# Making the rated feed-forward input in the first turn of the loop instead of the first two

## What is computed

```python
def conv_ffn(h, w_up, conv_w, conv_b, w_down):
    u = h @ w_up
    u = conv_b + sum(conv_w[j] * causal_shift(u, CONV_WIDTH - 1 - j) for j in range(CONV_WIDTH))
    gate, val = jnp.split(u, 2, axis=-1)
    return (jax.nn.silu(gate) * val) @ w_down
...
        x = x + conv_ffn(rms_norm(x, norm_ffn_g[l]), ffn_w_up[l], ffn_conv_w[l],
                         ffn_conv_b[l], ffn_w_down[l])
```

## Time and profile before

| what | us |
|---|---|
| median of 3 runs | 1028.18 (1027.68 to 1029.34) |
| the profiled execution | 1028.37 |
| its span, first to last instruction | 1026.6 |
| TensorE busy | 1008.1 (98%) |
| VectorE busy | 816.6 (80%) |
| ScalarE busy | 616.9 (60%) |

### The profile page before, as it was taken

One profiled execution on the slowest core, in us unless ns is written; L12 is line 12 of the kernel. 1 busy time (PEld: TensorE's weight loads), 2 busy tenths in 40 slices (PEclk: granted clock), 3 DMA queues, 4 the chain that ended last, 5 costly groups with the idle time before them and its releaser, 6 DMA issues.

```text
span 1026.6 us, 22212 instructions
## 1 busy us (share of the span) xinstructions
PE 1008.1 (98%) x8278; PEld 932.0 (91%) x8278; DVE 816.6 (80%) x1365; ACT 616.9 (60%) x967; POOL 11.9 (1%) x30
## 2 busy tenths in 40 slices
PE   8999999999999999999999999999999999999997
PEld 7998988899999999999999989789999999998886
DVE  6799763897797898878778996649977878888785
ACT  7964333656556665666689533246656565667665
POOL 0000000100000000000000000010000000000000
PEclk9999999999999999999999999999999999999999
DMA  8452342335545565555544534224445545565554
GB/s 301 148 182 103 104 146 81 114 111 178 162 154 179 180 209 183 189 185 184 191 142 145 185 99 144 88 74 142 139 153 167 182 164 185 172 219 185 192 192 152
DMA packets 46392, 164.42 MB, mean 160 GB/s; under 512 B 5888, under 2 KB 6064, under 8 KB 46304
## 3 DMA queue, kind: packets, MB, share of 16 engines
q1 hardware_dynamic: 44640, 160.19, 46.8%
q0 software_dynamic: 800, 1.33, 0.6%
q10 hardware_dynamic: 864, 1.63, 0.5%
HBM read 161.56 MB, written 1.05 MB: 158 GB/s over the span
## 4 chain that ended last, share of the span: by engine, by line
PE 86%; DVE 9%; ACT 2%; issue 2%; DMA 1%; SPq 0%; DVEq 0%; ACTq 0%
PE psum L471 85%; DVE sb_lo L1317 2%; ACT sb_rw L927 1%; DVE sb_inv L1566 1%; DVE sb_inv L1525 1%; DMA sb_x<-x_t 1%; DVE sb_inv L1528 1%; PE psum L789 1%; ACT sb_hh L927 0%; DVE sb_rw L1609 0%; DVE sb_yf L1590 0%; DVE sb_qb L1375 0%; ACT sb_hi L927 0%; DVE sb_rw L1496 0%; DVE sb_inv L1502 0%
## 5 line engine op out<-in xcount | busy, mean ns | idle before, releaser
L927 ACT ACTIVATE sb_hi<-sb_raw 128x1024 fp32r<-128x1024 f32 (+1 forms) x298 | 310.4, 1052 | 170.7 <-PE psum L471 161.2
L1317 DVE TENSOR_TENSOR sb_lo<-sb_raw,sb_hi 128x1024 fp32r<-128x1024 f32 x296 | 358.0, 1219 | 53.2 <-ACT sb_hi L927 52.9
L471 PE MATMUL psum<-sb_hh,sb_hi 128*128 128x256 f32 x1184 | 344.2, 291 | 3.2 <-DVE sb_hl L1324 2.1
L471 PE MATMUL psum<-sb_hl,sb_hi 128*128 128x256 f32 x1184 | 335.3, 283 | 0.0
L471 PE MATMUL psum<-sb_hh,sb_lo 128*128 128x256 f32 x1184 | 335.1, 283 | 0.0
L471 PE MATMUL psum<-sb_o,sb_hi 128*128 128x256 f32 (+1 forms) x1376 | 276.0, 314 | 1.3 <-DVE sb_o L1338 1.3
L471 PEld LDWEIGHTS psum<-sb_hh,sb_hi 128*128 128x128 f32 x1184 | 227.0, 192 | 17.9 <-issue 10.9
L471 PEld LDWEIGHTS psum<-sb_o,sb_hi 128*128 128x128 f32 x1376 | 224.1, 191 | 14.6 <-DVE sb_o L1338 1.7
L471 PEld LDWEIGHTS psum<-sb_hl,sb_hi 128*128 128x128 f32 x1184 | 227.3, 192 | 0.8 <-issue 0.5
L471 PEld LDWEIGHTS psum<-sb_hh,sb_lo 128*128 128x128 f32 x1184 | 227.2, 192 | 0.0
L471 PE MATMUL psum<-sb_o,sb_lo 128*128 128x256 f32 x880 | 193.9, 283 | 0.0
(11 more groups left out here) (187 smaller groups left out, 1027.7 us busy)
## 6 DMA issues: line engine op xcount, KB each, us to landing
sb_raw<-w_stream SPq DMA_DIRECT2D x299, 512.0 KB, 3.3
sb_pm<-mix_par ACTq DMA_DIRECT2D x2, 512.5 KB, 3.4
y_t<-sb_rw SPq DMA_DIRECT2D x4, 256.0 KB, 2.1
sb_cf<-const_f SPq DMA_DIRECT2D x1, 550.0 KB, 9.3
sb_pm<-mix_par SPq DMA_DIRECT2D x1, 512.5 KB, 10.9
sb_raw<-w_stream SPq DMA_DIRECT2D x2, 256.0 KB, 4.4
sb_x<-x_t ACTq DMA_DIRECT2D x2, 256.0 KB, 4.4
sb_x<-x_t SPq DMA_DIRECT2D x1, 512.0 KB, 6.7
```

Of the source, the lines that this page charges most:

```text
L471: return pe.matmul(out, lhsT, rhs, start=start, stop=stop, skip_group_check=True)
L927: return act.activation(out, in_, func, scale=scale, bias=bias, **kw)
L1317: tt(lo[:, s, :], raw[:, s, :], hi[:, s, :].bitcast(F32), ALU.subtract).then_inc(lo_done, 1)
```

## The change

`PLAIN_TURNS` goes from 2 to 1, so `RATED_FROM` goes from 10 to 6, and the loop of the program begins with the second turn. The rated input has to be ready four tiles earlier, and its steps move:

- `rate` 0 and 1 stand ahead of the first turn, 2 and 3 behind the product of tile 2, 4 and 5 behind that of tile 3, 6 and 7 behind that of tile 4.
- `rated_lo(l, 0)` stands behind `rate` 7 and `rated_lo(l, 1)` behind the product of tile 5.
- ScalarE's `rated_hi(l, 0)` stands between the two splits at the start of the second half of the first turn, `rated_hi(l, 1)` behind its product copy of tile 4.
- Tiles 6 to 9 go from `scale_up` to `low_half` and `add_up`.

```diff
-PLAIN_TURNS = 2
+PLAIN_TURNS = 1
...
-                        if halve:
-                            rated_hi(l, u // 2 - 1)
+                        if halve and u == 4:
+                            rated_hi(l, 0)
...
-
-                turn(0, False, False)
-                turn(1, False, True)
+                            if halve and u == 4 and r == 0:
+                                rated_hi(l, 1)
+
+                turn(0, False, True)
...
+                for k in range(2):
+                    rate(k)
                 before = own.n
...
-                                piece(i, u, r)
+                                piece(u, r)
...
-                def piece(i, u, r):
-
-                    if i == 0:
-                        first = 3 * (u // 2 - 1)
-                        for k in ((first,), (first + 1, first + 2))[r]:
-                            rate(k)
-                    elif u == 2 and r == 0:
-                        rated_lo(l, 0)
-                    elif u == 2:
-                        rate(6)
-                        rate(7)
-                    elif r == 1:
-                        rated_lo(l, 1)
+                def piece(u, r):
+
+                    for k in {(2, 0): (2, 3), (2, 1): (4, 5), (4, 0): (6, 7)}.get((u, r), ()):
+                        rate(k)
+                    if u == 4:
+                        rated_lo(l, r)
 
-                turn(0, False)
-                turn(1, False)
```

## The result

The changed kernel is slower by half a per cent: 1034.84 us in the median of 15 runs (1031.36 to 1038.50), where the kernel before takes 1029.34 in the median of its 15 (1027.68 to 1035.05). The ratio is 1.0053, with a 95% interval from 1.0041 to 1.0065. The difference of the medians, 5.5 us, is more than the 3.8 us of the forecast, and the time lies 0.9 us above the range. The three runs of the kernel before that stood ahead of the prediction (1028.18 in the median) lie 1.2 us under the median of these 15. Both kernels scatter by several microseconds, and that scatter turns out to be a part of the story.

A forecast was written before the change was run, and what follows sets the result against it. TensorE was taken to bound the kernel, with VectorE lacking slack in layer 0's first turn. The sum was 1028.37 + 3.29 + 1.70 - 1.36 = 1032.0 us, range 1031.0 to 1033.9.

The forecast's parts named there:

- What bounds the kernel, and the two engines side by side: TensorE has 86% of the span; VectorE is busy 30.24 of 31.00 us in layer 0's first turn, without slack.
- The saving of 1.36 us: Tiles 6 to 9 go wide in both layers: four pairs of tiles at 0.34 us each saved on TensorE.
- slab 7's delay: In layer 0, two rates ahead of the first turn make slab 7's low part 0.12 us later, counted within the wait.
- (a) to (d): Layer 0's first turn: moved rates and first low half delay VectorE 2.06 us; second half begins at 374.77, ends at 375.99.
- The wait of layer 1: At tile 6 of layer 1, TensorE waits for the second low half: 1.70 us lost, 2.07 with the pause.
- The pause of the earlier trace: Layer 1, before the product after tile 5: 0.46 us, about 0.37 more than usual, taken as an accident and left out.
- The wait: TensorE's first wide matmul at tile 6 waits for the second low half: 3.29 us lost in layer 0, 1.70 in layer 1.
- The sum without the clock: Whole kernel: 1028.37 + 3.29 + 1.70 - 1.36 = 1032.0 us, with chance 0.52.
- the clock: A fall to half rate in layer 0's wait at tile 6, estimated at 1.2 us (0 to 1.7), left out of the sum.
- R1: Rival: the clock falls in layer 0's wait, giving 1033.2 us, or 1034.4 if in both layers; chance 0.36.
- R2: Rival: TensorE finds the rated input ready or nearly at tile 6, so not slower, 1027.0 to 1028.4 us; chance 0.05.
- R3: Rival: layer 1's VectorE gaps swallow the added work, only layer 0's 3.29 us loss stands, giving 1030.3 us; chance 0.07.

The follow-up runs named there:

- e11_early_again: Changed kernel with the second low half made right behind the first in both layers, repeated beside the changed kernel on one chip: median 1028.03 us.
- e1_steps: Changed kernel with its moved steps, but tiles 6 to 9 kept plain: median 1028.96 us, ratio 1.0007 to the kernel before.
- e2_wait: Changed kernel with its moved steps, tiles 6 to 9 plain, but TensorE waiting for both low halves at tile 6: median 1035.19 us.
- e3_fill: Changed kernel with useless matmuls in front of the wait at tile 6, 24 in layer 0 and 12 in layer 1: median 1033.77 us.
- e12_after_again: The changed kernel once more, unaltered, beside other kernels on one chip: median 1033.29 us in nine runs.
- e7_wait_l0: Changed kernel with the second low half made early in layer 1 alone, the wait at tile 6 staying in layer 0: median 1033.78 us.
- e9_fill12: Changed kernel with 12 useless matmuls in front of the wait in layer 0 and none in layer 1: median 1033.44 us.
- e5_shift: Kernel before with useless matmuls in front of tile 6, 27 in layer 0 and 14 in layer 1: median 1037.03 us.
- e8_pool: Changed kernel with the eight rates made on GpSimd instead of VectorE, order of the low halves kept: median 1036.83 us.
- e10: Changed kernel with 6 useless matmuls in front of the wait in layer 0 and none in layer 1: median 1033.86 us.

## Why the prediction was right or wrong, point by point

**What bounds the kernel, and the two engines side by side**: right. VectorE is the engine that came late, from the lack of slack in the first turn of layer 0 (30.30 of 31.00 us busy there now).

**The saving of 1.36 us**: near. With the wait out of the way the two parts give 0.58 and 0.63 (e11_early_again), 1.21 together. With the 0.21 us that slab 7's delay takes in the two layers (e1_steps) added back, that is 1.42. The forecast counted slab 7's delay as a part of the wait, which is right for the changed kernel.

**VectorE's delay, (a) to (d)**: right in layer 0, where the second half began at 374.77 as said. The wait of layer 1 is worth 1.71 us (e2_wait), predicted 1.70. The pause of the earlier trace rows was rightly left out: after the change the product of tile 5 there (887.02) starts 0.59 us after the instruction before it, as in layer 0 (0.58).

**The wait**: 3.27 us measured with e3_fill, 3.29 predicted. The sum without the clock, 1032.0, is what an undisturbed execution takes (1032.3 in e12_after_again), and the level at equal clock is 3.7 and 3.3 us over the kernel before, where 3.6 was predicted.

**The step that failed is the clock.** The prediction left it out of the sum and gave its rival 0.36, on the ground that no row showed a wait of this length between dense stretches. It should have been the likeliest case: the row at the kernel's end had the clock fall 2.2 us after the last matmul, and the wait of layer 0 is longer. The price was too small as well. Estimated at 1.2 and bounded at 1.7 us, it was 1.56 in the changed kernel, 2.5 in e2_wait and 2.8 in e7_wait_l0. In the last two the spell began some 0.7 us before the wait ended, where the prediction expected it to cost less than 1.7, and it lasted twice as long as the one in the earlier trace rows. The rule of the Trainium skill that was cited beside this rival (TensorE: Matmul & The Clock Gate, "Why this matters for your kernels") was borne out in four of five profiled executions with the full wait.

This alone doesn't lead out of the range: R1 with 1.56 in place of 1.2 would be 1033.6. In the profiled execution the second fall, 1.57 us in the mixing part, does: 1032.0 + 1.56 + 1.57 = 1035.1, measured 1035.25. For that one the prediction had no term. In the medians the two can't be told apart. With the clock held in the wait of layer 0 they are still 5.2 and 4.6 us over the kernel before (e3_fill, e9_fill12), and the changed kernel is 4.4 over it in e12_after_again. So how much of the miss is the fall at the wait and how much lies elsewhere stays open.

**And the sum took the rest of the kernel as fixed.** It was made against one execution of 1028.37 us and a median of three. But the clock also falls in the mixing, behind runs of 64x64 matmuls with pauses between them: in the profiled executions at about 160 us (four of them) and at 665 to 674 us (seven), and at the start in nine of fourteen. The profile of the kernel before has only the fall at the start and that behind the last matmul, but its runs have mean clocks from 0.989 to 0.999, so it isn't spared. Its median moved by 1.2 us between 3 and 15 runs, and the changed kernel's mean clock is lower, 0.9942 where the kernel before has 0.9960 to 0.9968 in the three groups of the table. At 0.67 us for 0.001 that is 1.2 to 1.7 us, which with the 3.7 makes the 5.5 measured, nearly. The range ended at 1033.9 since it allowed only for falls at the two waits. That the time lay just outside it is in part the draw of executions, as the 1033.29 of the nine runs more shows; and that the sum was met to 0.3 us is worth something only for an execution without a fall.

**The rivals**: R2 (not slower) and R3 (only layer 0) are out, by the waits in both layers. R1's fall was there in most of the profiled executions.

**What stays open.** A spell that begins between 665 and 674 us is in the profiled executions of the changed kernel, e2, e3, e5, e7, e8 and e9, all of them delayed by the feed-forward part of layer 0, but not in e10 and e12, which are delayed as well. Whether the delay makes it likelier isn't settled by these runs; e5_shift was meant to tell and had too few. Nor is it known what decides, with the same wait, whether the clock falls.

## What to carry to other kernels

When a shared input is made earlier, follow the queue of the engine that makes it instruction by instruction up to the last piece, and compare its end with the moment at which the consumer arrives; an engine that is behind at the entry of a loop has no room for it there, however idle it is a turn later. Before giving up such a change, try the order: here the last piece moved ahead of one tile's work removed both waits and with them the loss of 3.7 us at equal clock, and by the traces left a gain of 1.2 us. And where TensorE gets a new wait as long as that of layer 0 here, count a fall of the clock into its price, and widen the range by the falls that come elsewhere in some executions.

## What the runs showed of the hardware

- TensorE's clock fell to half after waits of 2.2 us and more (2.17, 2.89 to 3.14 us by the profile) in five of six profiled executions, and in none of those of 1.3 to 1.6 us (layer 1, e9_fill12). It came between 1.3 us before TensorE's next matmul (e8_pool) and 1.4 us behind it (the changed kernel). It cost 1.56 us where the clock was low for 3.4 us, and 2.5 and 2.8 us where it was low for 6.8 (e2_wait, e7_wait_l0), beside the 3.27 us of the wait itself.
- In different executions of one kernel the clock falls at different places (the changed kernel and e12_after_again). The mean granted clock of a run explains most of the scatter: 0.67 us for 0.001, with 0.95 us of scatter left.
- GpSimd's multiplications of two SBUF operands doubled the time of VectorE's small instructions beside them (0.48 to 0.96 us, 0.42 to 0.95 us), but not of one that read PSUM (0.41). Its multiplications of one SBUF operand left most of them as they were.
